# Unread products given up at the head and in the normalising of the mixer's token groups

## What is computed

```
def rwkv7_branch(p, ...):
    ...                                   # r, decay, k, v, a, g from projections
    y = wkv7_scan(rh, decay, kh, vh, -kk, kk * ah)          # S = S*w + (S a) b^T + v k^T ; y = S r
    mean = jnp.mean(y, axis=-1, keepdims=True)              # per head of 64
    var = jnp.mean(jnp.square(y - mean), axis=-1, keepdims=True)
    y = ((y - mean) * lax.rsqrt(var + LNX_EPS)) * lnx_w + lnx_b
    bonus = jnp.sum(rh * kh * r_k, axis=-1, keepdims=True) * vh
    return (y + bonus) * g

def s5_branch(u, ...):
    ...                                   # complex linear scan over 512 tokens, 32 groups
    y = jax.nn.gelu(...)
    return y * jax.nn.sigmoid(y @ w_glu + b_glu)
```

## Time and profile before

| | |
|---|---|
| median of 3 runs | 3420.62 us |
| profiled execution, time | 3418.15 us |
| profiled execution, first to last instruction (span) | 3416.3 us |
| PE busy | 3257.5 us (95%) |
| PE weight loads busy | 2334.9 us (68%) |
| DVE busy | 1501.7 us (44%) |
| ACT busy | 809.0 us (24%) |
| POOL busy | 861.2 us (25%) |
| mean granted TensorE clock | 0.988 |

### The profile page before, as it was taken

One profiled execution on the slowest core, in us unless ns is written; L12 is line 12 of the kernel. 1 busy time (PEld: TensorE's weight loads), 2 busy tenths in 40 slices (PEclk: granted clock), 3 DMA queues, 4 the chain that ended last, 5 costly groups with the idle time before them and its releaser, 6 DMA issues. The chain is left out here.

```text
span 3416.3 us, 39707 instructions
## 1 busy us (share of the span) xinstructions
PE 3257.5 (95%) x15466; PEld 2334.9 (68%) x15466; DVE 1501.7 (44%) x2662; ACT 809.0 (24%) x1789; POOL 861.2 (25%) x537
## 2 busy tenths in 40 slices
PE   8999999999999999999999999989899999999998
PEld 7857757764444686776666544458677766788886
DVE  5575502331111565646654111143687622455552
ACT  3363211021111344432321111121222211211100
POOL 4214122310000430311003100014255231253352
PEclk9999999999999999999999999999899999999999
DMA  4251121147888322022232688861101122122221
GB/s 153 105 235 50 74 98 75 50 171 292 323 321 305 127 84 89 25 99 105 98 136 99 255 324 321 325 252 72 72 29 54 64 86 99 50 74 89 84 99 50
DMA packets 50270, 470.77 MB, mean 138 GB/s; under 512 B 5792, under 2 KB 6176, under 8 KB 26400
## 3 DMA queue, kind: packets, MB, share of 16 engines
q1 hardware_dynamic: 27072, 379.00, 29.9%
q0 software_dynamic: 21136, 78.39, 5.8%
q10 hardware_dynamic: 1872, 10.75, 0.8%
HBM read 506.65 MB, written 63.18 MB: 167 GB/s over the span
## 5 line engine op out<-in xcount | busy, mean ns | idle before, releaser
L638 PE MATMUL bank<-B,ring 128*128 128x256 f32 x4336 | 951.5, 380 | 18.7 <-DVE B L739 5.5
L638 PEld LDWEIGHTS bank<-B,ring 128*128 128x128 f32 x4336 | 823.6, 190 | 140.3 <-issue 27.6
L622 POOL TENSOR_TENSOR ring<-ring 128x1024 f32<-128x1024 f32 x58 | 148.8, 2565 | 1213.6 <-DMA ring<-in_w_static 383.0
L2056 PE MATMUL bank<-ring,B 128*128 128x512 f32 x960 | 419.1, 594 | 0.3 <-issue 0.3
L770 ACT ACTIVATE B<-bank 128x256 f32<-128x256 f32 x356 | 135.2, 384 | 963.5 <-PE bank L638 961.3
L2056 PEld LDWEIGHTS bank<-ring,B 128*128 128x128 f32 x960 | 180.2, 190 | 218.8 <-issue 218.8
L638 PE MATMUL bank<-XT,ring 128*128 128x256 f32 x1344 | 307.7, 383 | 22.8 <-DMA ring<-in_w_static 15.3
L541 PE MATMUL bank<-B,ring 128*128 128x512 f32 x704 | 305.6, 592 | 4.6 <-DVE B L1457 3.5
L638 PEld LDWEIGHTS bank<-XT,ring 128*128 128x128 f32 x1344 | 257.7, 192 | 64.2 <-issue 29.2
L541 PEld LDWEIGHTS bank<-B,ring 128*128 128x128 f32 x704 | 133.5, 190 | 166.0 <-issue 163.9
L2131 DVE TENSOR_TENSOR B<-B,bank 128x512 f32<-128x512 f32 x46 | 31.6, 688 | 467.4 <-PE bank L2056 407.8
(11 more groups left out here) (501 smaller groups left out, 4036.3 us busy)
## 6 DMA issues: line engine op xcount, KB each, us to landing
ring<-in_w_expert SPq DMA_DIRECT2D x96, 2048.0 KB, 9.2
ring<-in_w_static SPq DMA_DIRECT2D x79, 2048.0 KB, 8.4
B<-in_w_expert SPq DMA_DIRECT2D x42, 2048.0 KB
slots_y<-B POOLq DMA_DIRECT2D x52, 512.0 KB, 27.7
B<-slots_x POOLq DMA_DIRECT2D x44, 512.0 KB
slots_x<-B POOLq DMA_DIRECT2D x23, 512.0 KB, 16.3
ring<-s_tables SPq DMA_DIRECT2D x4, 2048.0 KB, 8.5
s_tables<-tmp POOLq DMA_DIRECT2D x8, 512.0 KB, 3.3
```

What stands on the lines that cost most here:

```text
L622: pool.tensor_tensor(s(0), w(1, 0), w(1, 1), ALU.add).then_inc(made.up(), 1)
L638: ins = pe.matmul(out, left, right, start=start and k == 0, stop=k == 3, skip_group_check=not start)
L2056: ins = pe.matmul(bank[:, :], xbT[q % 2][:, k, :], slot[:, k, :], start=k == 0, stop=k == KT - 1)
```

## The change

At the head of each of the four groups the wait for the vacant bank and the 7 unread products go (the same wait stands again a few lines further down, ahead of the first squaring). In the normalising of each of the four groups the 5 unread products ahead of L2641 and the 2 ahead of L2650 go. Nothing else is changed; the other calls of `hold_clock` stay, among them 3 or 10 ahead of each state of the last group, 3 ahead of the last `centre` and 7 ahead of `glu`.

```diff
             def square_round(tg, rnd, par):
                 if rnd == 0:
-                    if par == 0:
-                        pe.wait_ge(*bk.vacant(("sq", tg, rnd, par)))
-                        hold_clock(m, pe, bk.bank(("sq", tg, rnd, par)), 7)
                     pe.wait_ge(*bk.read_done(("LT", tg, par)))
                     pe.wait_ge(*bk.read_done(("L", tg, par)))
                 else:
...
             def spread_rstd(tg):
                 pe.wait_ge(*bk.vacant(("gv", tg)))
                 bank = bk.bank(("gv", tg))
-                hold_clock(m, pe, bank, 5)
                 pe.wait_ge(*m.tally("row_squares").at(tg + 1))
                 for ct in range(4):
                     ins = pe.matmul(bank[:, 2 * ct:2 * ct + 2], ysq[:, tok(ct)], head_cols, start=True, stop=True)
                 ins.then_inc(bk.full_sem(("gv", tg)), 1)
                 pe.wait_ge(*bk.vacant(("gb", tg)))
                 bank = bk.bank(("gb", tg))
-                hold_clock(m, pe, bank, 2)
                 pe.wait_ge(*m.tally("row_rstd").at(tg + 1))
```

## The result

| | before | after |
|---|---|---|
| median, both taken in turn on one chip | 3420.52 us (13 runs, 3416.52 to 3425.05) | 3427.08 us (13 runs, 3423.62 to 3431.01) |
| profiled execution, time | 3418.15 us | 3426.82 us |
| span | 3416.3 us | 3425.1 us |
| PE busy | 3257.5 us | 3255.2 us |
| mean granted clock | 0.988 | 0.984 |

The change made the kernel slower: ratio 1.0021, 95% interval [1.0013, 1.0028], which is 6.6 us (4.4 to 9.6). The time lies inside the predicted range, 4.4 us above the predicted value. The 112 records are gone (15466 to 15354 on PE), and PE was busy only 2.3 us less for it.

What follows compares the result with a forecast made beforehand. In the four groups' turns it took the round trip through DVE and ACT as the bound, hiding the products. Clock losses 0 + 2 × 0.46 + 1.0 + 0.2 = 2.1 us on the median 3420.62 gave 3422.7 us, range 3418 to 3428.

Steps and rivals of the forecast that it cites:

- The price of the products themselves: Heads and normalising: removing the products wins nothing direct, 0, at best −0.1 us at heads 0 and 1.
- The reading of the bank: Heads 0 and 1: L2486 writes the bank L2908 reads, so PE hands its win over there; if wrong, −1.43 us.
- The rival by which 1.43 us arrive: Heads 0 and 1: L2486 is late for another reason than DVE and the clock holds; 3419.2 us, chance 0.06.
- The heads of groups 2 and 3: The wait for DVE grows from 1.13 to about 2.8 us and squaring starts when it does now; price 0.
- the list of what to look for: Signs in the profile after, among them 2.5 to 2.8 us idle at heads 2 and 3, released by L3010.
- the case of the text in which the low stretch lies on the transposes: Next group's transposes and Gram products: up to 1.66 us more, fitting into the 2.8 us wait at heads 2 and 3.
- The rival that the clock falls at the heads as well: Squarings behind heads 2 and 3 run low, 3.3 us more; sum 5.4, 3426.0 us; chance 0.16, half beyond 0.2%.
- the argument against it: Heads 2 and 3: a late L2559 behind a low stretch fills the gap, making a fall at the head less likely.
- the term for the normalising: Clock falls about once per normalising: 0.46 us each in groups 0 and 1, 1.0 in group 2, 0.2 in group 3.
- The range: 3418 to 3428 us: from the second rival with the spread of runs to the third rival between its two sums.
- The sum's own bound from above: Normalisings: L2650 low in three groups 2.8, the 20 records in full 2.1, 0.9 in the last group; 5.8 us.
- The chance of 0.90 for a change within 0.2%: Whole run: same 0.90, faster 0.02, slower 0.08, where 0.2% is 6.8 us.

Runs made afterwards that it cites:

- heads alone: Kernel before with only the 7 unread products at each of the four heads removed, normalising kept: 3427.87 us against 3419.55, ratio 1.0025.
- the heads with waits: Kernel before with the 7 unread products of each head replaced by 54 already satisfied waits, code length kept: 3422.94 us against 3420.34, ratio 1.0014.
- the narrow products: Kernel before with the 5 and 2 unread products of each normalising 2 columns wide instead of 128: 3429.31 us against 3419.41, ratio 1.0029.
- the waits: Kernel before with all unread products that the change gives up replaced by satisfied waits of the same code length: 3427.77 us against 3420.34, ratio 1.0024.
- the pair of single removals: Kernel before with only the 5 products of each normalising removed, 3426.70 us, ratio 1.0026; with only the 2 removed, 3423.58 us, ratio 1.0013.
- the wide kernels: Kernel before with unread products in fewer, wider instructions, no column fewer: in the normalising 3423.93 us, ratio 1.0008; at the heads too 3429.66 us, ratio 1.0027.
- the 2 alone: Kernel before with only the 2 unread products ahead of the spreading product removed: 3423.58 us, 4.0 us more, ratio 1.0013.
- narrow heads: Kernel before with the 7 unread products of each head 2 columns wide, normalising as before: 3420.26 us against 3419.41, ratio 1.0003.
- more products: Kernel before with three products' columns more in each normalising (7 and 3 times 128), no instruction more: 3419.37 us, ratio 0.9998.
- narrow at both places: Kernel before with all 14 unread products of each group, heads and normalising, 2 columns wide: 3428.78 us against 3419.41, ratio 1.0025.

## Why the prediction came out as it did

**The price of the products themselves** was right: nothing in the normalising, where the waits behind them took over what they left. At the heads of groups 0 and 1 the squaring starts 2.88 us after its Gram products begin where it was 3.65, 0.77 earlier (0.78 and 0.65 predicted). I had that all but 0.1 would be lost again at L2486. From the Gram products to it, it is 8.37 us at head 0 against 8.66, and 8.78 against 9.03 at head 1, so 0.29 and 0.25 came through, 0.54 us in all. The reading of the bank was right: L2486 still starts 0.05 us behind DVE's row for it at both heads (at head 0 that row, L2903, ends at 2488.23). What came through lies in DVE's own rows, which took 8.32 us from the Gram products to there at head 0 and 8.61 before. The rival by which 1.43 us arrive was wrong for the most part.

**The heads of groups 2 and 3** went as argued, not as the list of what to look for had it. An idle time of 2.5 to 2.8 us is not there; it is 0.82, because the clock is low on the transposes ahead. That is the case of the text in which the low stretch lies on the transposes and the head pays it: from transposes to squaring it is 6.49 and 6.63 us against 6.84. The rival that the clock falls at the heads as well did not come true: the low stretches end ahead of the squarings, and the gap that was to bring it is short, as the argument against it had it. With the normalising left whole the clock can fall there: it is low behind both heads in the trace of heads alone, not in that of the heads with waits, and 0.0013 to 0.0015 lower over the executions in the two kernels that have no work there.

**The step that failed** is the term for the normalising: "I cannot tell where in the normalising the fall lands, so half: 0.46 us each in groups 0 and 1." That the clock falls there was right. The size supposed one short low stretch that hits L2650 or misses it; the row sums L2641 and the S5 products behind L2650 were in no term. The stretch is 13.5 us long and covers everything from L2630 to the Gram products. By the starts in order of time, group 0 pays 0.87 us from L2637 to L2645, 0.88 from L2645 to the S5 products behind it, and 0.95 from those to the transposes; group 1 pays 0.54 ahead of L2637 as well. That is 2.7 and 3.2 us in place of 0.46 each. Group 2 cost 1.25 + 1.76 = 3.0 in place of 1.0 (it was put at half of 2.1, and L2645 not counted), group 3 0.55 in place of 0.2. Together 9.5 us in place of 2.1. I had a row for it: the low stretch that the trace of before shows around the transposes of group 0; I used its factor and did not ask how long it lasts once the work in it is thin and waits.

Against the 9.5 stand the 0.54 of the heads 0 and 1, 0.56 (0.35 + 0.21) at the heads 2 and 3, and 1.66 that the change did not earn, luck of the two executions: in this execution the transposes of group 0 ran at full clock (1.97 us, 3.63 before). The stalls among the chunk products are 1.1 us longer (2.64 against 1.49). That makes 9.5 - 0.54 - 0.56 - 1.66 + 1.1 = 7.8, and the stage shows 7.5. The other 1.3 us of the spans' difference lie behind it: the clock is at 0.50 for 3.41 us from 2757.39 on, in the stage that follows.

**The range** held by luck. Its upper end was set by the rival of the heads, and 3426.0, the sum of that rival, is nearest to the measured 3427.08, but its mechanism did not come about. The sum's own bound from above was 5.8 us, and 6.6 (4.4 to 9.6) were measured, three times the 2.1 forecast. The chance of 0.90 for a change within 0.2% was too high: the ratio of 1.0021 lies at that border.

**What the runs left standing.** That the loss of this change is the clock in the normalising: shown, by the narrow products (nothing moved, 9.9 us) and by the waits (as many instructions as before, 7.4 us). That the 5 products carry most of it: supported by the pair of single removals and by the clock of their executions, not shown, since the intervals overlap. What my theory did not have: that the heads' products, harmless in the sum, cost 8.3 us when they alone are taken out. Part of it goes with the clock (3.9 us by the line); the rest is of the size of the stalls. That these come from code which stands elsewhere is not settled. For it speak the wide kernels; against it, that with the code in its old places stalls of 1.92 to 2.83 us stand in group 3 too. Whether the 2 alone lose by the clock or by a stall that brings the clock down is open: their trace has both. And at one and the same place of the code, group 3's stall was 0.16 us (before), none (narrow heads, narrow normalising) and 1.92 to 2.83 us (more products, narrow at both places, waits). In each of the ten traces with a stall of 1.9 us or more there, a packet of the instruction queue lands 1.4 to 1.6 us before the stall ends, among the loads of weights; whether these delay the packet was not tried apart. Nor is it settled why narrow products at the heads cost the clock 0.0002 and empty heads 0.0013 to 0.0015, while in the normalising narrow is as bad as none. No version beat the kernel before.

## What to carry to other kernels

Work with no result can be what holds the clock: before taking it out of a wait, ask how long a low stretch would last in what is left, not only whether one begins. Thin products and round trips between engines did not bring the clock back here for 13.5 us, and PE's products in that chain took up to 1.9 times as long (3.67 us for 1.97). And when instructions are removed, put the same number of others in their place in one experiment: it keeps what the work was worth apart from what the code's new place may cost.

## What was not expected of the hardware

PE counted as busy in every moment of 13.50 us and had a clock of 0.50 throughout (narrow products in the normalising). The Trainium skill (TensorE: Matmul & The Clock Gate, Part 1) says that how busy the engine has lately been sets the clock; these rows show that the profile's busy time is not the measure of it, since with 128 columns PE was busy 4.89 of 5.70 us in the normalising of group 1 and the clock was 1.00.

PE also waited where no other engine was late: up to 3.82 us among small products. The Trainium skill (Runtime: NRT & Kernel Launch, Instruction fetch mechanics) says that instructions come in blocks over a DMA queue of their own and that issuing is slow enough to hide it. Around the stall of 3.70 us with the heads' products gone, from 2710 us on, the traffic by queue (packets, MB, share of 16 engines) was:

```profile
q1 hardware_dynamic: 67, 0.88, 62.1%
q8 instruction: 1, 0.02, 1.6%
```

The one instruction packet falls into the stall, beside 67 packets of weights. If the fetch is the cause, it is not hidden here; that rests on the coincidence in time, which is the same in all ten traces with such a stall.
